# A two-block transformer on one core: inner values of the first mixture turned by VectorE, four lanes in the second mixture, a longer ring of weights

## The chip, the cores and the metric

The kernel runs on one core of one Trainium2 chip. The metric is the device time of an execution in microseconds; before the change the median of three runs is 2532.16 us (2531.34 to 2532.30).

The engines are named as in the profile: PE is TensorE's matmul row and PEld its weight loads, DVE is VectorE, ACT ScalarE, POOL GpSimd, SP SyncE. The queue of SP issues all the loads of weights (SPq).

## What is computed

Two blocks follow each other on 256 tokens of 1024 channels, all in float32: a block of two layers (attention and a dense feed-forward; attention and a mixture of 8 experts with 3584 inner columns, top 2) and a second block (a recurrence and a dilated attention beside each other, then a mixture of 32 experts with 512 inner columns in 4 groups, top 2 within the best group). What the change touches are the two mixtures and what lies just before the second:

```python
def moe_swiglu(h, router_w, w_gate, w_up, w_down):          # first mixture, E = 8, F = 3584
    t = h.reshape(B * S, D)
    logits = (t @ router_w).astype(jnp.float32)
    top_v, top_i = lax.top_k(logits, TOP_K)
    top_w = jax.nn.softmax(top_v, axis=-1)
    gates = jnp.sum(jax.nn.one_hot(top_i, N_EXPERTS) * top_w[..., None], axis=1)
    for e in range(N_EXPERTS):
        y = y + gates[:, e:e + 1] * swiglu(t, w_gate[e], w_up[e], w_down[e])

def swiglu(h, w_gate, w_up, w_down):
    return (jax.nn.silu(h @ w_gate) * (h @ w_up)) @ w_down

def hier_moe(h, ...):                                       # second mixture, E = 32, F = 512
    grp_logits = h @ w_router_group + b_router_group
    grp = jnp.argmax(grp_logits, axis=-1)
    exp_logits = (h @ w_router_expert + b_router_expert).reshape(N, 4, 8)[tok_idx, grp]
    top_v, top_i = lax.top_k(exp_logits, 2)
    gate = softmax(grp_logits)[grp] * jax.nn.softmax(top_v, axis=-1)
    # each token goes through its two experts: (silu(x @ w_gate[e]) * (x @ w_up[e])) @ w_down[e]
```

## The kernel before

Activations are held with channels on the partitions (`x_chan`, `h_chan`: 128 x 8 x 256). Weights come from one stream of slots of 128 x 2048 floats (1.0486 MB) into a ring of 14 slots in SBUF. `Loads.load` (L128) makes SP wait until the slot's last user has counted up `used` and issues one DMA per slot; `Loads.ready` makes the reader wait for the arrival. The order of the loads on SP's queue is the order of the code.

Each stage is a block of five engine programs; a block ends for all engines together. The stages are: setup, mixer 0, dense, mixer 1, route and first mixture (`stage_route` L1097, `stage_blocks` L1490), the hybrid stage (front, attention, recurrence, merge), route and second mixture (`stage_route` again, `stage_lanes` L1806).

**Routing.** `stage_route` scales the activations, multiplies them with the router's weights (L1140), transposes them to tokens on the partitions (L1148, ACT copies them to `h_tok`), finds the first two experts of each token on DVE (L1176 to L1211), and numbers the tokens of each expert (`place`). `fullest` is the number of tokens of the fullest expert. `pick_slots` (L1241) turns places into 0/1 matrices, and a matmul of `h_tok` with them gathers an expert's tokens (L1344, L1704).

**Overflow.** A mixture's main pass gives each expert a fixed width, 96 tokens in the first, 64 in the second. If `fullest` is above it, an `If` in each engine runs all the further rounds of that width up to 256 tokens, each with all the weights again.

**First mixture.** `BlockWork.pe_expert` (L1396) takes one expert at a time. The expert's 96 tokens are three blocks of 32. For each slot of weights TensorE runs 3 x 4 matmuls (L1368), each with 32 tokens as the stationary operand in one quarter of the array's columns, so that partition 32 i + token of a bank holds the inner columns of quarter i. The 3584 inner columns go in two spans, 4 x 512 (slots 0 to 15, gate then up) and 4 x 384 (slots 16 to 31). ACT takes the SiLU, DVE the product (`hidden`, L1479). For the down projection the inner columns must lie on partitions: `pe_flips` (L1373) transposes `hidden` on TensorE in pieces of 128x128, 12 for the wide span and 9 for the narrow one, and DVE copies them from PSUM to `turned` (L1484). The down slots 32 to 45 follow (L1390, 24 matmuls of 256 columns a slot), with the next expert's gather between.

**Second mixture.** `LaneWork.pe_group` (L1719) takes two experts (lanes) at a time, 64 tokens each, in the two halves of the columns: 8 slots of gate and up weights (L1722), a gather for the next group (L1704), 4 transposes of `hidden` (L1733), 4 slots of down weights (L1749), and the spread of the results back to all tokens (L1760), which DVE adds up (L1800). 16 groups use 192 slots; the inner 14 are a loop on each engine. Its ring has 12 of the 14 slots. SP issues the first 12 loads at the start of the second route's block (`loads.head`) and the others in the mixture's block.

**Merge.** `hybrid_merge` (L2527) is the last block ahead of the second route: the two branches are projected (L2559, L2591), gated, and multiplied with `w_out` (L2606, four slots). SP loads the router and the last two `w_out` slots there.

## Time and profile before

| | |
|---|---|
| median of 3 runs | 2532.16 us |
| profiled execution | 2534.23 us |
| its span | 2532.1 us |
| PE busy | 2452.8 us (97%) |
| DVE busy | 768.9 us (30%) |
| ACT busy | 327.4 us (13%) |
| moved from HBM | 716.54 MB |
| mean granted TensorE clock | 0.993 |

The span runs from the first to the last instruction of the profiled execution. A matmul in float32 leaves two records in the trace, a transpose one. PE counts as busy while a matmul is under way, so its share does not say how full the array is; matmuls in different quarters of the columns run beside each other, and their durations add up to more than the busy time. PEclk is the granted clock as a share of 2.4 GHz.

### The profile page before, as it was taken

How to read it: one execution, taken by the hardware profiler on the slowest of the kernel's cores; microseconds unless marked ns; L12 is line 12 of the kernel's file. 1: busy time of each engine (PE TensorE's matmuls, PEld its weight loads, DVE VectorE, ACT ScalarE, POOL GpSimd, SP SyncE). 2: the span in 40 equal slices, each digit the busy share in tenths (PEclk: the TensorE clock that was granted, in tenths of full speed). 3: DMA queues.
4: the chain of work that ended last, by engine and by line, in shares of the span. 5: the costliest groups of instructions: out<-in, count | busy, mean ns of one | idle time of the engine just before them, and what ended most of it. 6: DMA issues, size and time to landing. Idle time of an engine off the chain costs nothing. (4 is left out here: it accounts for less than half of the span.)

```text
span 2532.1 us, 50359 instructions
## 1 busy us (share of the span) xinstructions
PE 2452.8 (97%) x22858; PEld 1545.7 (61%) x22858; DVE 768.9 (30%) x1341; ACT 327.4 (13%) x728; POOL 14.5 (1%) x12
## 2 busy tenths in 40 slices
PE   6999999999999999999999999999999999999999
PEld 5678888867453535353535353688789864444444
DVE  6762222436201010111111111345465342222222
ACT  3430000243100000000000000233232110000000
POOL 1000000100000000000000000000000000000000
PEclk9999999999999999999999999899999999999999
DMA  9566554605699999999999999333300179999998
GB/s 399 212 271 252 216 216 199 251 1 233 244 364 364 369 362 371 361 375 353 378 355 379 357 377 351 136 123 139 130 3 4 37 330 406 422 422 421 422 422 354
DMA packets 105238, 720.68 MB, mean 285 GB/s; under 512 B 11952, under 2 KB 12624, under 8 KB 30416
## 3 DMA queue, kind: packets, MB, share of 16 engines
q1 hardware_dynamic: 105040, 717.67, 71.5%
q8 instruction: 169, 2.77, 0.4%
q14 instruction: 29, 0.24, 0.0%
HBM read 716.54 MB, written 1.05 MB: 283 GB/s over the span
## 5 line engine op out<-in xcount | busy, mean ns | idle before, releaser
L1368 PE MATMUL bank<-ring,moe_xg 128*32 128x512 f32 (+1 forms) x6144 | 582.3, 539 | 6.1 <-DVE moe_acc L1468 5.5
L1368 PEld LDWEIGHTS bank<-ring,moe_xg 128*32 128x32 f32 x6144 | 197.8, 110 | 378.1 <-issue 367.8
L1390 PE MATMUL bank<-ring,moe_turned 128*32 128x256 f32 x5376 | 296.1, 379 | 0.0
L1390 PEld LDWEIGHTS bank<-ring,moe_turned 128*32 128x32 f32 x5376 | 172.3, 110 | 116.1 <-issue 4.4
L1722 PE MATMUL bank<-ring,moe_shared 128*64 128x512 f32 x1024 | 223.5, 594 | 0.8 <-DVE moe_shared L1773 0.8
L1057 PE MATMUL bank<-h_chan,ring 128*128 128x256 f32 x896 | 195.6, 379 | 1.4 <-ACT h_chan L482 1.4
L1057 PEld LDWEIGHTS bank<-h_chan,ring 128*128 128x128 f32 x896 | 170.2, 190 | 24.7 <-issue 1.6
L1722 PEld LDWEIGHTS bank<-ring,moe_shared 128*64 128x64 f32 x1024 | 72.0, 137 | 142.6 <-issue 141.6
L2199 PE MATMUL bank<-h_chan,ring 128*128 128x256 f32 x672 | 149.7, 383 | 1.9 <-DVE h_chan L2304 1.9
L1479 DVE TENSOR_TENSOR moe_hidden<-moe_silu,bank 128x512 f32<-128x512 f32 (+1 forms) x48 | 26.9, 616 | 395.0 <-PE bank L1368 395.0
L2199 PEld LDWEIGHTS bank<-h_chan,ring 128*128 128x128 f32 x672 | 128.2, 192 | 23.6 <-issue 6.3
L1749 PE MATMUL bank<-ring,moe_turned 128*64 128x512 f32 x512 | 113.4, 595 | 0.8 <-DVE moe_turned L1785 0.8
L1041 PE MATMUL bank<-dense_hidden,ring 128*128 128x256 f32 x448 | 98.8, 379 | 0.0
L1041 PEld LDWEIGHTS bank<-dense_hidden,ring 128*128 128x128 f32 x448 | 85.1, 190 | 11.6
L580 PE MATMUL bank<-h_chan,ring 128*128 128x256 f32 x384 | 85.1, 380 | 1.0 <-ACT h_chan L482 1.0
L1454 DVE COPY moe_y<-bank 32x256 f32<-32x256 f32 x48 | 19.9, 415 | 209.5 <-PE bank L1390 209.0
L1437 ACT ACTIVATE moe_silu<-bank 128x512 f32<-128x512 f32 (+1 forms) x48 | 22.6, 544 | 471.0 <-PE bank L1368 471.0
L580 PEld LDWEIGHTS bank<-h_chan,ring 128*128 128x128 f32 x384 | 72.5, 190 | 15.0 <-issue 5.4
L1749 PEld LDWEIGHTS bank<-ring,moe_turned 128*64 128x64 f32 x512 | 35.3, 137 | 66.8 <-issue 64.0
L1447 ACT ACTIVATE moe_y<-bank 32x256 f32<-32x256 f32 x48 | 18.1, 377 | 441.0 <-PE bank L1390 440.5
L1781 DVE TENSOR_TENSOR moe_hidden<-moe_silu,bank 128x512 f32<-128x512 f32 x16 | 11.0, 688 | 201.8 <-PE bank L1722 201.8
L1074 DVE TENSOR_TENSOR dense_hidden<-dense_silu,bank 128x512 f32<-128x512 f32 x14 | 9.6, 687 | 201.3 <-PE bank L1057 201.3
(408 smaller groups left out, 2436.5 us busy)
## 6 DMA issues: line engine op xcount, KB each, us to landing
ring<-stream SPq DMA_DIRECT2D x313, 1024.0 KB, 13.8
ring<-wide SPq DMA_DIRECT2D x240, 1024.0 KB, 7.2
ring<-wide SPq DMA_DIRECT2D x128, 768.0 KB, 6.0
ada_slots<-stream SPq DMA_DIRECT2D x28, 1024.0 KB, 6.9
x_chan<-xT SPq DMA_DIRECT2D x1, 1024.0 KB, 14.9
ring<-lora SPq DMA_DIRECT2D x1, 1024.0 KB, 6.5
out<-x_chan SPq DMA_DIRECT2D x4, 256.0 KB, 2.1
hyb_work<-dilated SPq DMA_DIRECT2D x1, 768.0 KB, 8.9
```

The source lines that it names most:

```text
L580: mm = nc.tensor.matmul(b[:, 0:T], w[:, t, i * P:(i + 1) * P], k.hT[:, t, :], start=(t == 0), stop=(t == DT - 1))
L1041: mm = nc.tensor.matmul(k.bank[t // 2][:, (t % 2) * T:(t % 2) * T + T], w[:, f, t * P:(t + 1) * P], hidden[:, c % 2, f, :], start=(c == 0 ...
L1057: mm = nc.tensor.matmul(b[:, f * T:(f + 1) * T], w[:, t, f * P:(f + 1) * P], k.hT[:, t, :], start=(t == 0), stop=(t == DT - 1))
L1368: mm = self.k.nc.tensor.matmul(banks[r][i * TILE:(i + 1) * TILE, 0:width], self.m.xg[:, t, r * TILE:(r + 1) * TILE], w[:, i, :], start=(t ...
L1390: mm = self.k.nc.tensor.matmul(self.sum_bank[r][q * TILE:(q + 1) * TILE, :], self.m.turned[:, r, 4 * c + f, i * TILE:(i + 1) * TILE], w[:, ...
L1437: k.nc.scalar.activation(m.silu[:, r, 0:self.span[c]], self.gate_bank[r][:, 0:self.span[c]], ACT.Silu)\
L1447: last = self.k.nc.scalar.activation(self.m.y[r * TILE:(r + 1) * TILE, q * T:(q + 1) * T], self.sum_bank[r][q * TILE:(q + 1) * TILE, :], A ...
L1454: last = self.k.nc.vector.tensor_copy(self.m.y[r * TILE:(r + 1) * TILE, q * T:(q + 1) * T], self.sum_bank[r][q * TILE:(q + 1) * TILE, :])
L1479: v.tensor_tensor(m.hidden[:, r, 0:self.span[c]], m.silu[:, r, 0:self.span[c]], self.up_bank[r][:, 0:self.span[c]], ALU.mult).then_inc(*se ...
L1722: mm = k.nc.tensor.matmul((self.gate_bank if j < self.per_proj else self.up_bank)[own, :], m.xg[:, t, own], w[:, i, e, :], start=(t == 0), ...
L1749: mm = k.nc.tensor.matmul(k.bank[half][own, :], m.turned[:, f, own], w[:, i, e, :], start=(f == 0), stop=(f == 3))
L2199: mm = nc.tensor.matmul(b[:, 0:T], lhsT, rhs, start=(t == 0), stop=(t == DT - 1))
```

## The change

- *First mixture.* `pe_flips` is gone. DVE turns `hidden` into `turned` with its own transpose, which turns each block of 32x32 in place of the grid, SBUF to SBUF, one instruction per block of tokens and span. The down weights' rows are put in the order that this gives, on the host. TensorE waits for the products (`hidden_ready`) before the second narrow projection and before down slot 35, and for `turned_ready` where it waited for the copies.
- *Second mixture.* Its width falls from 64 to 32 tokens, so four experts share the array's columns: 8 groups, each with 16 slots of gate and up weights and 8 of down weights, still 192 slots. All groups are written out, with no loop. The overflow rounds are seven instead of three.
- *Ring.* Two more slots (`late`) lie in the memory that the hybrid stage uses as `work`; the second mixture's ring has 16 slots in the order `LAST_ORDER`. SP issues its loads 0 to 14 in the merge's block, between the last loads of the hybrid stage, and load 15 in the route's.
- *Routes.* The logits are computed with the router's weights as the stationary operand (8 matmuls with 256 columns instead of 16), copied by DVE and transposed to tokens in two pieces between the other transposes. `acc` is cleared after the mask, not before the first step. The gate weights move out of the route's block to behind the first gather's copies (`gate_weights`), and the first `pick_slots` moves into it.
- *Merge.* Temporaries lie elsewhere; the arithmetic is the same.

```diff
-RING = 14
+RING, LATE = 14, 2
@@ Loads
-        p = j % self.slots
+        p = self.order[j % self.slots]
@@ stage_route
-                for tok in range(TT):
-                    mm = nc.tensor.matmul(k.bank[1][:, tok * R:(tok + 1) * R], k.hT[:, t, tok * P:(tok + 1) * P],
-                                          router_w[:, t, :], start=(t == 0 and tok == 0), stop=(t == DT - 1),
-                                          skip_group_check=True)
-            mm.then_inc(*pe_step.up())
+                mm = nc.tensor.matmul(k.bank[4][0:R, 0:T], router_w[:, t, :], k.hT[:, t, :], start=(t == 0),
+                                      stop=(t == DT - 1))
+            mm.then_inc(*S("logits_done").up())
...
+                if n == 2:
+                    pe.wait_ge(*S("logits_out").at(1))
+                    for half in range(TT):
+                        mm = nc.tensor.transpose(k.bank[1][:, half * R:(half + 1) * R],
+                                                 logit_rows[:, half * P:(half + 1) * P], k.t("ident")[0:R, 0:R])
+                    mm.then_inc(*pe_step.up())
...
-            link(v.memset(m.acc[:, :, :], 0.0))
+            dve.wait_ge(*S("logits_done").at(1))
+            v.tensor_copy(logit_rows, k.bank[4][0:R, 0:T]).then_inc(*S("logits_out").up())
             dve.wait_ge(*pe_step.at(1))
...
-            dve.wait_ge(*S("exp_done").at(1))
-            link(v.tensor_scalar(col("w1"), col("w"), 1.0, None, ALU.add))
...
-            link(v.tensor_tensor(m.gates[:, :, :], col("hot1", E), col("hot2", E), ALU.add))
+            link(v.memset(m.acc[:, :, :], 0.0))
             dve.wait_ge(*pe_step.at(2))
...
+            pick_slots(k, m, first, link)
@@ BlockWork.pe_expert
-        self.pe_project(pe, g, 16, self.gate_bank, NARROW, range(2))
-        self.pe_flips(pe, g, 0)
-        self.pe_project(pe, g, 16, self.gate_bank, NARROW, range(2, DT))
+        self.pe_project(pe, g, 16, self.gate_bank, NARROW)
+        pe.wait_ge(*self.hidden_ready.at(g * 6 + 3))
         self.pe_project(pe, g, 24, self.up_bank, NARROW)
-        pe.wait_ge(*self.flip_out.at(g * 6 + 3))
+        pe.wait_ge(*self.turned_ready.at(g * 6 + 3))
         for j in range(32, 46):
-            if j == 34:
-                self.pe_flips(pe, g, 1)
+            if j == 35:
+                pe.wait_ge(*self.hidden_ready.at(g * 6 + 6))
...
             if j == 40:
-                pe.wait_ge(*self.flip_out.at(g * 6 + 6))
+                pe.wait_ge(*self.turned_ready.at(g * 6 + 6))
@@ BlockWork.dve_expert
-                dve.wait_ge(*self.flip_done.at(g * 6 + (3 * c + r + 1)))
-                n = self.parts[c]
-                v.tensor_copy(m.turned[:, r, 4 * c:4 * c + n, :], self.flip_bank[3 * c + r][:, 0:n * P].rearrange(
-                    "p (f n) -> p f n", f=n)).then_inc(*self.flip_out.up())
+                dve.wait_ge(*self.hidden_ready.at(g * 6 + (3 * c + r + 1)))
+                f0 = c * WIDE
+                v.transpose(m.turned[:, r, f0:f0 + self.span[c]], m.hidden[:, r, 0:self.span[c]])\
+                    .then_inc(*self.turned_ready.up())
@@ stage_lanes, TensorE
-            main.pe_group(pe, 0, True)
-            main.pe_spread(pe, 0)
-            with pe.Fori(1, G - 1) as g:
-                main.pe_group(pe, g)
-                main.pe_spread(pe, g)
-            main.pe_group(pe, G - 1, False, True)
+            for g in range(G):
+                main.pe_group(pe, g, g == 0, g + 1 == G)
+                if g + 1 < G:
+                    main.pe_spread(pe, g)
@@ hybrid
+LAST_ORDER = [5, 6, 8, 9, 10, 11, 12, 13, RING, RING + 1, 7, 1, 2, 3, 4, 0]
+ISSUED = 15
@@ hybrid_merge, SP
-            for j in range(ATTN_OUT + HYBRID_RING, loads.n):
+            for j in range(4):
+                nxt.load(sp, j)
+            loads.load(sp, ATTN_OUT + HYBRID_RING)
+            for j in range(4, 10):
+                nxt.load(sp, j)
+            sp.wait_ge(*loads.done(ATTN_OUT))
+            nxt.load(sp, 10)
+            for j in range(ATTN_OUT + HYBRID_RING + 1, loads.n):
                 loads.load(sp, j)
+            for j in range(11, ISSUED):
+                nxt.load(sp, j)
@@ program
-                ("hybrid", 31, HYBRID_RING, 1), ("moe2", 12, 12, 16)]
+                ("hybrid", 31, HYBRID_RING, 1), ("moe2", 192, RING + LATE, 1)]
...
-                m = Mixture(k, stage, "moe2", 32, C, "router2", 36, True)
+                m = Mixture(k, stage, "moe2", 32, QUAD_SLOTS, "router2", 36, True,
+                            k.late[:, LATE, :].rearrange("p (t n) -> p t n", t=TT))
@@ host
+def turned_rows(down):
+
+    wide = down[:QUADS * WIDE].reshape(QUADS, WIDE // TILE, TILE, D)
+    narrow = down[QUADS * WIDE:].reshape(QUADS, NARROW // TILE, TILE, D)
+    return np.concatenate([part.transpose(1, 0, 2, 3).reshape(-1, D) for part in (wide, narrow)])
```

TensorE's order in the first mixture, one expert from its wide up projection to its last down slots; before (L1379 are the transposes, L1368 the projections, L1390 the down slots, L1344 the gather):

```order
L1368 MATMUL bank<-ring,moe_xg 32x512 x96
L1368 MATMUL bank<-ring,moe_xg 32x384 x24
L1379 MATMUL bank<-tab_sb,moe_hidden 128x128 x12
L1368 MATMUL bank<-ring,moe_xg 32x384 x168
L1390 MATMUL bank<-ring,moe_turned 32x256 x48
L1379 MATMUL bank<-tab_sb,moe_hidden 128x128 x9
L1390 MATMUL bank<-ring,moe_turned 32x256 x24
L1344 MATMUL bank<-moe_pick,moe_h_tok 128x96 x8
L1390 MATMUL bank<-ring,moe_turned 32x256 x24
```

and now:

```order
L1391 MATMUL bank<-ring,moe_xg 32x512 x96
L1391 MATMUL bank<-ring,moe_xg 32x384 x192
L1402 MATMUL bank<-ring,moe_turned 32x256 x72
L1367 MATMUL bank<-moe_pick,moe_h_tok 128x96 x8
L1402 MATMUL bank<-ring,moe_turned 32x256 x24
```

The two runs of transposes are gone, and the projections and down slots around them close up; nothing else moves.

SyncE's queue from the merge's block to the start of the second mixture's, before (`ring<-stream` is a slot of weights; the first two are `w_out`'s, the twelve belong to the mixture):

```order
L2546 DMA ring<-router 128x288
L2547 DMA ring<-router_b 128x36
L136 DMA ring<-stream 128x2048 x2
L2543 UNCONDITIONAL_BRANCH
L1112 UNCONDITIONAL_BRANCH
L136 DMA ring<-stream 128x2048 x12
L1111 UNCONDITIONAL_BRANCH
```

and now (`late<-stream` are the two new slots; among the seventeen in the merge's block two are `w_out`'s, the fifth and the thirteenth):

```order
L2553 DMA late<-router 128x288
L2554 DMA mod<-router_b 128x36
L138 DMA ring<-stream 128x2048 x9
L138 DMA late<-stream 128x2048 x2
L138 DMA ring<-stream 128x2048 x6
L2550 UNCONDITIONAL_BRANCH
L1123 UNCONDITIONAL_BRANCH
L138 DMA ring<-stream 128x2048
L1122 UNCONDITIONAL_BRANCH
```

Fifteen of the mixture's loads now stand in the merge's block and one in the route's.

TensorE in the second mixture, its first group, before (L1722 gate and up, L1277 gate turns, L1704 gather, L1733 transposes, L1749 down, L1760 spread):

```order
L1722 MATMUL bank<-ring,moe_shared 64x512 x16
L1277 MATMUL bank<-tab_sb,h_chan 128x128 x16
L1722 MATMUL bank<-ring,moe_shared 64x512 x16
L1277 MATMUL bank<-tab_sb,h_chan 128x128 x16
L1704 MATMUL bank<-moe_pick,moe_h_tok 128x128 x8
L1733 MATMUL bank<-tab_sb,moe_hidden 128x128 x4
L1704 MATMUL bank<-moe_pick,moe_h_tok 128x128 x8
L1749 MATMUL bank<-ring,moe_turned 64x512 x16
L1760 MATMUL bank<-moe_gate_t,moe_shared 128x256 x8
```

and now:

```order
L1737 MATMUL bank<-ring,moe_shared 32x512 x32
L1300 MATMUL bank<-tab_sb,h_chan 128x128 x8
L1737 MATMUL bank<-late,moe_shared 32x512 x8
L1737 MATMUL bank<-ring,moe_shared 32x512 x24
L1300 MATMUL bank<-tab_sb,h_chan 128x128 x8
L1719 MATMUL bank<-moe_pick,late 128x128 x8
L1748 MATMUL bank<-tab_sb,moe_hidden 128x128 x4
L1719 MATMUL bank<-moe_pick,late 128x128 x8
L1764 MATMUL bank<-ring,moe_turned 32x512 x32
L1775 MATMUL bank<-moe_gate_t,moe_shared 128x256 x8
```

The gate and up matmuls of a group are 64 of 32 columns where they were 32 of 64, the down matmuls 32 where they were 16; gather, transposes and spread of a group are as many as before, for four experts instead of two.

## Rows read from the trace of the kernel before

**Rows 1.** The page, its head.

```profile
span 2532.1 us, 50359 instructions
```

**Rows 2.** Busy time per engine in stretches (us busy, records; then PEclk, DMA share, GB/s).

```profile
1100.00:1200.00 100.00, 98.78 (x1216) 44.59 (x1219) 10.23 (x18) 5.09 (x12) 0.00 (x0) 1.00 0.94 359
...
2200.00:2300.00 100.00, 100.00 (x511) 47.49 (x511) 25.98 (x39) 1.79 (x3) 0.00 (x0) 1.00 1.01 422
2500.00:2540.00 40.00, 27.21 (x124) 11.35 (x124) 9.89 (x12) 0.60 (x1) 0.00 (x0) 0.97 0.57 232
```

**Rows 3.** SyncE's queue, waits from 700 to 1560 us (total, times, longest).

```profile
SPq L188 <- PE bank L1368: 482.7, 201, 6.6
```

**Rows 4.** TensorE's timeline, first mixture (start, duration, line, operation, count).

```profile
940.22 1.09 PE L1379 MATMUL bank<-tab_sb,moe_hidden 128*128 128x128 f32 x8
...
942.30 27.30 PE L1368 MATMUL bank<-ring,moe_xg 128*32 128x384 f32 x336
...
974.71 1.20 PE L1379 MATMUL bank<-tab_sb,moe_hidden 128*128 128x128 f32 x9
975.84 2.80 PE L1390 MATMUL bank<-ring,moe_turned 128*32 128x256 f32 x48
...
1061.15 1.09 PE L1379 MATMUL bank<-tab_sb,moe_hidden 128*128 128x128 f32 x8
```

**Rows 5.** The chain that ended last, second mixture (start, duration, what).

```profile
2063.83 7.09 PE bank L1722 x32
...
2096.65 13.88 PE bank L1722 x64
...
2125.60 13.88 PE bank L1722 x64
...
2143.68 7.02 PE bank L1749 x32
...
2154.54 13.88 PE bank L1722 x64
```

**Rows 6.** Stretch at the head loads' start.

```profile
2038.00:2040.00 2.00, 1.86 (x16) 1.67 (x15) 1.67 (x1) 0.29 (x1) 0.00 (x0) 1.00 0.38 115
```

**Rows 7.** Groups by line, 1000 to 1100 us (busy us, mean ns of one; idle before).

```profile
L1368 PE MATMUL bank<-ring,moe_xg 128*32 128x512 f32 (+1 forms) x768 | 72.8, 539 | 0.8 <-DVE moe_acc L1468 0.8
...
L1484 DVE COPY moe_turned<-bank 128x512 f32<-128x512 f32 (+1 forms) x6 | 3.5, 619 | 6.9 <-PE bank L1379 6.9
```

**Rows 8.** Timeline of the second route.

```profile
2040.12 3.26 DVE L476 SCALAR_TENSOR_TENSOR h_chan<-x_chan,vec_sb,rstd 128x256 f32<-128x256 f32 x8
...
2043.75 1.76 DVE L1168 MEMSET moe_acc<- 128x2048 f32 x1 [0.38 <-issue]
...
2044.37 3.48 PE L1148 MATMUL bank<-tab_sb,h_chan 128*128 128x128 f32 x16
...
2045.55 0.17 DVE L1191 TENSOR_TENSOR moe_gl<-bank,ring 128x8 f32<-128x8 f32 x1
...
2052.04 0.22 DVE L1211 TENSOR_TENSOR moe_chosen<-moe_hot 128x64 f32<-128x64 f32 x1
...
2057.41 2.93 PE L1704 MATMUL bank<-moe_pick,moe_h_tok 128*128 128x128 f32 x12 [1.03 <-DVE moe_pick L1241]
```

**Rows 9.** Timelines of the merge, SyncE's queue and TensorE.

```profile
1994.45 7.24 SPq L136 DMA_DIRECT2D ring<-stream  x2
...
2008.07 27.79 PE L2606 MATMUL bank<-h_chan,ring 128*128 128x256 f32 x128
```

**Rows 10.** Groups by line, second mixture.

```profile
L1722 PE MATMUL bank<-ring,moe_shared 128*64 128x512 f32 x1024 | 223.5, 594 | 0.8 <-DVE moe_shared L1773 0.8
```

**Rows 11.** Timeline of the kernel's end.

```profile
2525.12 3.72 PE L1889 MATMUL bank<-moe_gate_t,moe_shared 128*128 128x256 f32 x16
```

**Rows 12.** Stretches behind the first mixture.

```profile
1610.00:1615.00 5.00, 2.32 (x37) 1.27 (x26) 2.49 (x6) 2.26 (x6) 0.00 (x0) 0.91 0.02 3
1615.00:1620.00 5.00, 4.63 (x12) 3.49 (x11) 2.08 (x5) 1.81 (x5) 0.00 (x0) 0.50 0.03 7
```

More of the change, by code:

```diff
@@ L115, with __init__ @@
 class Loads:
-    def __init__(self, ring, n, slots=RING, turns=1):
+    def __init__(self, ring, n, slots=RING, turns=1, order=None):
         assert turns == 1 or n % slots == 0
@@ L146, in ready @@
     def ready(self, pe, j, turn=0):
[L148 removed]
+        p = self.order[j % self.slots]
         per = self.n // self.slots if self.turns > 1 else 0
@@ L225, in __init__ @@
         self.ring = sb("ring", [P, RING, SLOT])
-        self.weights = self.new_ring("slot", [self.ring[:, p, :] for p in range(RING)])
+        self.weights = self.new_ring("slot", [self.ring[:, p, :] for p in range(RING)] + [None] * LATE)
         self.used = self.weights.used
@@ L1114, in _ @@
             if loads is not None:
-                loads.head(sp)
+                for j in range(ISSUED, loads.slots):
+                    loads.load(sp, j)
         @block.scalar
@@ L1809, in stage_lanes @@
     W = m.width
-    main = LaneWork(k, m, loads)
+    main = LaneWork(k, m, loads, False)
     G = m.experts // main.lanes
     k.family = family
-    more = [LaneWork(k, m, part) for part in again]
+    more = [LaneWork(k, m, part, True) for part in again]
     first = more[0]
@@ L2524, in hybrid_attention, with hybrid_merge @@
     k.close()
-def hybrid_merge(k, loads, rec, o, fin, gate, acc, nxt_norm):
+def hybrid_merge(k, loads, nxt, rec, o, fin, gate, acc, nxt_norm):
     nc = k.nc
@@ L2991, in program @@
             if RUN is None or name in RUN:
-                loads[name] = Loads(k.weights, n, ring, turns)
+                loads[name] = Loads(k.weights, n, ring, turns, LAST_ORDER if name == "moe2" else None)
                 if name == "ada":
```

150 lines of the change are left out of this document (74 added, 76 removed).

## The prediction

> **What bounds the kernel now.** I read the page first (span, throttle, transfer rate), then the stage table, then TensorE's timeline in the first mixture, the chain of waits in the second, and the joints between. Three stages matter. The profiled execution took 2534.2 us, of which 2532.1 is span [rows 1] and 2.1 lie around it; the median, 2532.2, is 2.1 below it.
>
> The first mixture (646 to 1610 us) is bound by TensorE. Its busy time is 98.8 of 100 us at full clock, beside transfers at 359 GB/s [rows 2], and in 860 us of it SyncE's queue waited 482.7 us for a projection to give a slot back [rows 3]. One expert's first transposes start at 940.22, the next one's at 1061.15: 120.93 us [rows 4], and the same holds for the other inner experts.
>
> The second mixture (2063.8 to 2525) stands close to two limits at once. TensorE's chain has no gap: a group of two experts takes 2154.54 - 2125.60 = 28.94 us [rows 5], and there are 16. The transfers run at 422 GB/s with a DMA share of 1.01 [rows 2], the highest sustained in the trace; a slot of 1.0486 MB is then 2.485 us, and a group's twelve slots 29.8 us. TensorE gets along with less than that only because the twelve slots loaded ahead are slowly used up. The last bytes: 232 GB/s times 40 us is 9.28 MB after 2500 [rows 2], less 1.05 MB of output, so 19.5 us at 422: the last weights land near 2519.5.
>
> Between them the DMA engines are nearly idle, until SyncE's head loads begin to flow about 2039.4 (a DMA share of 0.38 in 2038 to 2040 [rows 6]).
>
> **First mixture.** Removed: 21 TensorE transposes per expert. They cost TensorE 940.22 to 942.30 (12 of them with the wait for the bank between) and 974.71 to 975.84 (9): 2.08 + 1.13 = 3.21 us, times 8 experts = **25.7 us**, all on the path. Also removed are six copies PSUM to SBUF per expert on DVE (619 ns mean [rows 7]).
>
> Added: six DVE transposes of 128x512 or 128x384, SBUF to SBUF. The trace of before has none. From below, the nearest row is that copy, 0.62 us; from above I allow 1.9 us, three times it. The place decides nothing up to far more: the first three have the whole narrow projections, over 30 us, to finish in; the second three start about 2 us after the last projection and must be done by down slot j = 40, eight down slots (2.80 us each [rows 4]) and two gathers after the last projection, some 25 us. Three transposes of up to 7 us each are hidden. I take 0. The two new waits on the products (before the second narrow projection, and at down slot j = 35) come 15 us and 8 us after the matmuls that feed them, while three products, of the copies' size, take some 2 us: 0. Behind DVE's transposes stand only the takes for the next expert, needed 25 us later. The order of the down weights is changed on the host: 0.
>
> With an expert at 117.7 us, the transfers must give 44.04 MB (3 x 1024 x 3584 floats) / 117.7 us = 374 GB/s instead of 364. The projections and down slots already draw faster than that between pauses, and 422 is shown elsewhere [rows 2]; 0.
>
> **Routes.** Logits are now computed turned (8 matmuls of 256 columns for 16 narrow ones), copied and turned back; the gate weights leave the route, the clearing of acc moves behind the mask, the first picks move ahead of the block's end. In the second route DVE's last scaling ended at 2043.38 and its first routing step came at 2045.55, right after the 1.76 us clearing [rows 8]. Now the step follows the last logit matmul (about 2044.2: wait, 0.44 of matmul, landing), half of the sixteen transposes (3.48 / 2 = 1.74 us) and two small ones: about 2046.2, **0.7 us later**. After it, the mask is done 6.7 us later as before (2045.55 to 2052.26), then 1.76 of clearing, 0.9 of places, 0.6 of picks, 1.8 of block change: 11.8 us, against 57.41 - 45.55 = 11.86. So +0.7 us to the first weight matmul, now 2064.5. In the first route the same steps end on TensorE's own queue (turns, ten warming matmuls, mask sums), which do not shrink: 0, bounds -1 and +1.
>
> **Prefetch.** SyncE issues slots 0 to 3 at the merge's start (1982), 4 to 14 between w_out loads, slot 15 in the route: 16 instead of 12, all landed by about 2042. What is passed: the third w_out slot goes out at 1994.45 as before [rows 9], the fourth behind seven mixture slots. Even if all nine land in turn, 1994.5 + 1 + 9 x 2.485 = 2017.9; TensorE reads it after three quarters of 27.79 us, at 2028.9 [rows 9]. 11 us of cover: 0. Without that cover TensorE would wait for it in the merge and everything after would shift.
>
> **Second mixture.** With four lanes of 32 columns, a slot is four matmuls (0.87 us) instead of 1.74, if four narrow matmuls overlap as two wide ones did. The first mixture's do: a record of 448 columns in the mean costs it 72.8 / 768 = 0.095 us [rows 7], or 0.108 at 512, half of the second's 223.5 / 1024 = 0.218 with two lanes [rows 10]; a matmul leaves two records, so a slot is 8 x 0.108. A group now covers four experts and 24 slots, and TensorE needs for it again 28.94 us (13.88 up, 7.02 down, the rest gathers, turns, spread [rows 5]) while its transfers take 24 x 2.485 = 59.6. So the **transfers alone** set the end. Gather, spread and DVE halve behind them: 0. The refill begins when the first slot is free, 2064.5 + 0.87 = 2065.4, flows 1.5 us later (as the head did: route block 2037.9, flow 2039.4), and has 192 - 16 = 176 slots: 437.4 us, last landing 2504.3. Before, it was 2519.5. The last slot then costs 0.87 us and the tail 6.98 (2525.12 to 2532.1 [rows 11]) at full clock.
>
> The clock: after a stretch with TensorE busy 2.32 of 5 us the granted clock was 0.91, then 0.50 in the next 5 [rows 12]; 0.50 is 1.2 GHz. In the new stage TensorE has 0.87 us of work in each 2.485, so I expect 1.2 GHz near the end: the last slot 1.74 instead of 0.87, and two tail steps 0.9 more together. End 2504.3 + 0.1 + 1.7 + 7.9 = 2514.0, a gain of **18.1 us** in this stage with the route's 0.7 in it.
>
> [...]
>
> **Sum.** 2532.1 - 25.7 - 18.1 = 2488.3 span, 2490.4 for the profiled execution; for the median the two offsets of 2.1 cancel: **2488.3 us**.
>
> **Rivals.**
> 1. *The first mixture turns transfer-bound.* For it: share 0.94 at 359 GB/s [rows 2], as if little were left. Against: SyncE waits on TensorE, not the reverse [rows 3]. If so, the 25.7 us stay: 2514.
> 2. *TensorE at 1.2 GHz through the whole second mixture.* A group then takes 57.9 us, just under 59.6, so it never works off the lead: first group (2063.83 to 2096.65 before, 32.8 us, with the gate turns [rows 5]) 65.5, six groups 347.4, the last 44: 2064.5 + 457 = 2521.4, plus 7.9, less 25.7: about 2504. For it [rows 12]; against, full clock should return when work is dense.
> 3. *The other side: an expert with more than 32 tokens.* The width of the second mixture's main pass falls from 64 to 32; if any expert draws 33 or more, all seven overflow rounds run, each at least 192 slots of 2.485 us: 7 x 477 = 3340 us more, 5830 in all. The trace cannot show the fullest expert, only that it is at most 64. Working out the reference's routing for its own inputs gives 26 for the fullest of 32 (mean 16), which speaks strongly against it.
>
> **Chances.** Forecast 0.78, rival 1 0.06, rival 2 0.12, rival 3 0.04. A measurement of this kernel tells about 0.2% (5 us) from no change; none of the first three comes within that. Range: full clock at the end (-1.8), 425 instead of 422 GB/s (-3), routes (-1) and rounding give 2481; rival 2 gives 2504. Rivals 1 and 3 stay outside. Faster 0.94, within 0.2% 0.02, slower 0.04.
>
> **What would show it.** First mixture: expert to expert 117.7 us; DVE transposes well under 7 us with TensorE waiting for none. Merge: DMA share high from 1982, w_out matmuls still 27.8 us. Second mixture: 422 GB/s up to the last landing, groups 59.6 us apart, TensorE waiting on ring slots, the clock at 0.5 in parts. Wrong if the expert period stays near 120.9, if the transfers fall below 415 GB/s (each 1% is 4.4 us), or if overflow rounds appear.

## The result, and the profile after

The changed kernel takes **2486.4 us** (median of 4 runs, 2483.5 to 2489.9), the kernel before 2531.8 beside it (4 runs, 2530.9 to 2532.3): a ratio of 0.9822, with a 95% interval of 0.9805 to 0.9839. The forecast was 2488.3 in a range of 2481 to 2504. The profiled execution is the slowest of the four, 2489.9 us with a span of 2487.8; against the span of [rows 1] that is 44.3 us less, where the forecast had 43.8. The two numbers agree better than their parts do, so the parts come first.

The page of the changed kernel: its span, and in 40 slices TensorE's busy tenths, its granted clock, and the transfer rate.

```profile
span 2487.8 us, 47996 instructions
...
PE   6999999999999999999999999999999987776776
...
PEclk9999999999999999999999999999999998777777
...
GB/s 398 224 253 279 220 220 203 256 1 188 241 381 367 387 372 387 364 387 371 386 367 388 370 385 364 141 125 135 124 3 4 255 184 420 421 421 421 422 421 332
```

The first mixture (slices 12 to 25) still shows a full TensorE, now at 364 to 388 GB/s. In the last seven slices, the second mixture, TensorE is idle for a fifth to two fifths of the time, its clock is at seven or eight tenths, and the transfers stand at 421 until the last slice: what bounds the stage has changed hands.

The same in stretches, to be laid beside [rows 2] (us busy and records of TensorE, its weight loads, VectorE, ScalarE, GpSimd; granted clock, DMA share, GB/s):

```profile
1100.00:1200.00 100.00, 99.22 (x1216) 41.30 (x1204) 11.85 (x22) 5.09 (x12) 0.00 (x0) 1.00 0.97 379
2200.00:2300.00 100.00, 71.56 (x408) 22.18 (x400) 11.40 (x17) 0.60 (x1) 0.00 (x0) 0.76 1.01 421
```

TensorE's timeline over one inner expert of the first mixture, which answers to [rows 4] (start, duration, line, operation, count):

```profile
880.32 20.78 PE L1391 MATMUL bank<-ring,moe_xg 128*32 128x512 f32 x192
901.03 3.91 PE L1380 MATMUL bank<-moe_gate_t,moe_y 96*128 96x256 f32 x16
905.73 51.77 PE L1391 MATMUL bank<-ring,moe_xg 128*32 128x512 f32 x576 [0.79 <-DVE moe_acc L1479]
957.31 7.95 PE L1402 MATMUL bank<-ring,moe_turned 128*32 128x256 f32 x144
...
971.83 26.11 PE L1402 MATMUL bank<-ring,moe_turned 128*32 128x256 f32 x480
997.75 2.76 PE L1391 MATMUL bank<-ring,moe_xg 128*32 128x512 f32 x24
```

From 905.73 to 957.31 the projections run in one piece; before, 12 transposes with a wait stood in them, and 9 more in the down slots. An expert now takes 997.75 - 880.32 = 117.43 us, against 120.93: 3.50 us less. From the first gather to the closing products the eight experts took 968.1 us before and 940.1 now, 28.0 less. SyncE's queue still waits for TensorE and not the other way round; its waits from 700 to 1530 us (total, times, longest) answer to [rows 3]:

```profile
SPq L190 <- PE bank L1391: 464.5, 199, 6.6
```

What VectorE does in TensorE's place, grouped by line and shape from 700 to 1500 us (busy us, mean ns of one; idle before):

```profile
L1495 DVE STREAM_TRANSPOSE moe_turned<-moe_hidden 128x512 f32<-128x512 f32 x18 | 11.3, 682 | 0.0
L1490 DVE TENSOR_TENSOR moe_hidden<-moe_silu,bank 128x512 f32<-128x512 f32 x18 | 11.3, 683 | 125.6 <-PE bank L1391 125.6
```

A turn of 128x512 in 32x32 blocks takes 682 ns, as long as the product before it (128x384: 547 ns), and waits for nothing. The forecast's bounds for it were 0.62 and 1.9 us.

The end of the kernel, which answers to [rows 11] (start, duration, engine and operation, idle before and what ended it):

```profile
2471.91 1.77 PE L1764 MATMUL bank<-ring,moe_turned 128*32 128x512 f32 x8 [0.53 <-DMA ring<-stream]
...
2474.34 1.06 PE L1764 MATMUL bank<-ring,moe_turned 128*32 128x512 f32 x8 [0.66 <-DMA ring<-stream]
2475.47 0.69 DVE L1808 COPY moe_shared<-bank 128x512 f32<-128x512 f32 x1 [9.16 <-PE bank L1764]
...
2478.18 6.39 PE L1898 MATMUL bank<-moe_gate_t,moe_shared 128*128 128x256 f32 x16 [2.78 <-issue]
```

Two things are new here. Between the last slot and the closing products (line 1898) TensorE stands for 2.78 us and waits for nothing that the profile shows. And these products take 6.39 us instead of the 3.72 of [rows 11], the same 16 records.

**Where the 44.3 us lie**, by the starts of the same steps in the two traces:

| stretch | forecast | measured |
|---|---|---|
| start to the first gather of the first mixture (646.39, now 643.53) | 0 | -2.9 |
| eight experts of the first mixture | -25.7 | -28.0 |
| its closing products and the norm behind | 0 | -4.4 |
| hybrid stage up to the merge (mostly the recurrence) | 0 | +2.4 |
| merge and second route up to the first weight product | +0.7 | -0.4 |
| second mixture and tail | -18.8 | -11.0 |

The -4.4 are a clock: the eight closing products (16 records) take 3.72 us now, and 2.93 and 4.42 us in two pieces before, when the granted clock fell to 0.50 [rows 12]. They are not shown to belong to the change: in kernels with the change's code at this place the same products took 3.7, 5.4, 6.9 or 7.1 us. The +2.4 and the shortfall in the last row needed experiments.

### The profile page after: what moved, and what is told of

It reads as the page before. It is cut to its first block and busy times, and to the rows that moved or that the text cites. A ratio compares the mean times of both kernels' runs of the same rounds, so it can differ in the third digit from the quotient of the medians.

```text
span 2487.8 us, 47996 instructions
## 1 busy us (share of the span) xinstructions
PE 2289.4 (92%) x22230; PEld 1400.9 (56%) x22230; DVE 708.9 (28%) x1263; ACT 320.1 (13%) x716; POOL 14.5 (1%) x12
## 3 DMA queue, kind: packets, MB, share of 16 engines
q8 instruction: 178, 2.92, 0.5%
## 5 line engine op out<-in xcount | busy, mean ns | idle before, releaser
L1737 PE MATMUL bank<-ring,moe_shared 128*32 128x512 f32 x896 | 161.7, 818 | 79.6 <-DMA ring<-stream 78.8
L1737 PEld LDWEIGHTS bank<-ring,moe_shared 128*32 128x32 f32 x896 | 22.1, 123 | 210.2 <-DMA ring<-stream 196.0
L1764 PE MATMUL bank<-ring,moe_turned 128*32 128x512 f32 x448 | 71.1, 736 | 36.8 <-DMA ring<-stream 36.8
L1796 DVE TENSOR_TENSOR moe_hidden<-moe_silu,bank 128x512 f32<-128x512 f32 x8 | 5.5, 688 | 250.4 <-PE bank L1737 250.4
L312 DVE CUSTOM_DVE_ANT_0 ada_product<-ada_slots,ada_c 128x1024 f32<-128x1024 f32 x56 | 68.5, 1223 | 1.5
```

What stands on the lines that cost most here:

```text
L312: mul = k.nc.vector.tensor_tensor_reduce(product, w[:, i * D:(i + 1) * D], c_row, 1.0, 0.0, ALU.mult, ALU.add, accum_out=k.mod[:, l, at:at ...
L1737: mm = k.nc.tensor.matmul((self.gate_bank if j < self.per_proj else self.up_bank)[own, :], m.xg[:, t, own], w[:, i, e, :], start=(t == 0), ...
L1764: mm = k.nc.tensor.matmul(k.bank[half][own, :], m.turned[:, f, own], w[:, i, e, :], start=(f == 0), stop=(f == 3))
```

## Experiments

All have before measured beside them; "the change" is the changed kernel.

**1. The first mixture alone.** The kernel before with the new first mixture and its down weights; all else as it was.

```
+ v.transpose(m.turned[:, r, f0:f0 + span], m.hidden[:, r, 0:span])
- self.pe_flips(pe, g, 0)   (and the copies out of the flip banks)
+ turned_rows(down[e])      (the host's order of the down weights)
```

> The kernel before, with the new first mixture alone: inner values turned by the vector engine in 32x32 blocks, down weights in that order, no TensorE transposes; routes, merge and second mixture as before. If the gain of the first mixture is TensorE's own (the transposes it no longer issues, 28.0 us less in the trace of the change), it comes out here alone: 2503 to 2507 us, a ratio of 0.989 to 0.990. If the first mixture were bound by its transfers, or if its gain hung on the new route, this would stay at 2530 or above 2510. The 2.4 us that the change lost in the recurrence should be absent if they come from the changed buffers of the hybrid stage, and present if they come from where instructions lie in memory.

Measured: 2501.6 us (2500.5 to 2503.4), ratio 0.9884 (0.9868 to 0.9901), 29.9 us less, 1.4 us better than the range expected. The projections are in one piece again, and the eight experts take 940.1 us, as in the change. It is the larger part of the change and stands by itself. The recurrence took 352.0 us here, with the old buffers, so the changed buffers are not what makes it long.

```profile
907.08 51.77 PE L1368 MATMUL bank<-ring,moe_xg 128*32 128x512 f32 x576 [0.78 <-DVE moe_acc L1456]
```

**2 to 4. The loads ahead and the lanes, apart.** First, all sixteen first slots asked for in the route:

```
-ISSUED = 15
+ISSUED = 0        (and no nxt.load in hybrid_merge)
```

> The change without its loads ahead: none of the sixteen first slots of the second mixture is asked for in the merge, all sixteen at the start of the second route. If the second mixture is set by its transfers, all 192 slots then follow that point: 192 x 2.49 us from about 2009 us gives a last landing near 2487 instead of 2474 us, and a time of 2497 to 2500 us. If the merge's own wait gets shorter without those loads in its way, up to 4 us of it come back. If TensorE were the bound of the second mixture, nothing but the first slot's landing would count, and the time would stay within 2 us of the change, 2486.

Then eight of them in the merge:

```
-ISSUED = 15
+ISSUED = 8
```

> The change with only eight of the slots of the second mixture asked for in the merge and eight at the start of the second route. The route's 23 us hold the transfer of eight slots (8 x 2.49 = 19.9 us and a landing of about 2 us), so all sixteen are in when the first slot comes free: no change, 2484 to 2489 us. If instead every slot asked for in the merge counts, half of the loss of the kernel without loads ahead appears, about 6 us: 2492.

Then two lanes with the loads ahead:

```
-QUAD_SLOTS = 32
+QUAD_SLOTS = 64   (two late slots given up for tables)
```

> The change with two lanes of 64 tokens in place of four lanes of 32 in the second mixture, with the loads ahead kept (thirteen of fourteen slots, since the wider tables take the room of the two late slots). If TensorE's 28.94 us a group of twelve slots sets the pace again, sixteen groups take 463.0 us, and with the new start at 2030.6 and a tail of 6 to 10 us the time is 2499 to 2504 us. If the loads ahead alone made the gain and lanes did nothing, 2486 to 2489.

Measured: without loads ahead 2496.9 (ratio 0.9870, 0.9854 to 0.9887); eight ahead 2486.2 (0.9825, 0.9808 to 0.9841), the change's time; two lanes 2501.1 (0.9882, 0.9865 to 0.9898). The four kernels that have the new first mixture, side by side, medians in us (all but the first have the new routes too):

| | two lanes | four lanes |
|---|---|---|
| no loads ahead | 2501.6 | 2496.9 |
| loads ahead | 2501.1 | 2486.4 |

The first kernel has the old routes, and these alone cost it 3.0 us ahead of the first gather (see the routes below). So the 0.5 and 4.7 us that separate it from the next two are not the worth of loads or lanes. The traces tell them apart, by the time from the second mixture's first weight product to the end, in us:

| | two lanes | four lanes |
|---|---|---|
| no loads ahead | 468.3 | 468.8 |
| loads ahead | 470.6 | 457.2 |

The kernel before takes 468.3 there. Neither part gains anything alone; together they gain 11. The chain that ended last says why. In the two-lane kernel, from 2150 to 2200 us (start, duration, what), it is TensorE without a gap, a group every 29.00 us, so an earlier transfer has nothing to bring:

```profile
2149.99 13.88 PE bank L1737 x64
2163.87 1.98 PE bank L1719 x16
2168.08 7.02 PE bank L1764 x32
2177.03 1.97 PE bank L1775 x8
2178.99 13.88 PE bank L1737 x64
```

In the kernel without loads ahead it is the transfers. They run at 1.02 from before TensorE's first slot on, and all 192 slots lie behind the route's start; from the second gather to the last slot it takes 461.6 us, against 448.6 in the change. What the four lanes free before the last landing is lost again behind it: from the last slot's start to the end this kernel takes 12.1 us, where the kernel before takes some 8.7 (an estimate, with the start put at the last quarter of its 7.09 us of down products). Its stretches:

```profile
2020.00:2040.00 20.00, 18.35 (x156) 8.49 (x154) 7.54 (x17) 2.93 (x4) 0.00 (x0) 0.96 1.02 422
2040.00:2460.00 420.00, 301.63 (x1716) 89.27 (x1716) 50.04 (x71) 5.26 (x9) 0.00 (x0) 0.77 1.01 421
```

And eight slots ahead are as good as fifteen, because the route's 23 us move the other eight before TensorE gives the first one back. What counts is that sixteen have landed by then, not when they were asked for.

**5. The change again**, beside the next three on one chip.

> The changed kernel as it is, again, beside the next three on the same chip. 2483 to 2490 us. If the 2.4 us that its recurrence took longer (352.5 us from the first input product of the hybrid stage to the first product of the merge, against 350.1 before) belong to the change, it is 352 to 353 again; if it is a spread of the executions, anything from 348 to 353. The gap between the last slot and the closing products is again 1.7 to 2.8 us.

Measured: 2484.7 us (2483.8 to 2485.2), ratio 0.9814. The recurrence took 350.4 us, so the same kernel has it at 352.5 and at 350.4. Over all kernels with this very code it took 348.2 to 352.5 us. The +2.4 of the table are such a spread, not the change. Three TensorE gaps of 0.22 to 0.36 us put down to "issue", which this trace lacks, make 0.9 of the 2.0 us between the two; what makes them and the rest is open. The gap ahead of the closing products is there again, 2.92 us, just above the range expected.

**6 to 8. Who makes the gap?** Three edits on TensorE's queue. Twelve identity products ahead of the branch on the fullest expert:

```
+ keep_warm(k, k.bank[5], 12)
  with pe.If(fullest > W):
```

> The change with twelve identity products (128x128, 0.24 us each at the full clock) on TensorE between the last slot's products and the branch on the fullest expert. If the 2.8 us gap there is TensorE's sequencer at the branch while its array has nothing to do, and the 6.40 us of the closing products are the clock that fell in that gap, the filler runs inside the gap and the closing products take 3.7 us: about 2.7 us less than the change, 2483 to 2484. If the branch is decided only after the array has finished what is ahead of it, the filler adds its 2.9 us and the gap stays: 2487 to 2490.

TensorE's branch left out:

```
- with pe.If(fullest > W):
-     ...
```

> The change with TensorE's branch after the last group left out, and with it TensorE's part of the rounds for experts with more than 32 tokens, which these inputs do not need (the fullest has 26). If the gap before the closing products is the branch, reached only when the last slot has landed, it goes: the first closing products start within 0.1 us of the last slot's end, and the time from there to the end falls from 12.4 us to about 7 at the full clock or 9.6 at the half: 2.8 to 5.4 us less than the change, 2481 to 2484. If the gap is the vector engine's copy of the last sums, only the order inside the 12.4 us changes: 0 to 1 us less.

The branch ahead of the last group's down slots:

```
+ with pe.If(fullest > W):  down slots; extra rounds; closing products
+ with pe.Else():           down slots; closing products
```

> The change with TensorE's branch moved ahead of the last group's eight down slots: both sides of the branch hold those slots and the closing products, and the one for full experts also the extra rounds, so nothing is left out. The branch then costs its 2 to 3 us where TensorE idles 0.5 to 1.4 us a slot for transfers anyway and catches up within a few slots. Same as with the branch left out: 2.8 to 5.4 us less than the change, 2481 to 2484. If an Else costs a jump before the closing products too, or code has to be fetched there, the gap stays and it is no faster than the change.

Measured: filler 2488.0 us (2484.0 to 2489.6), no branch **2479.1** (2477.8 to 2483.9; 5.6 less than experiment 5, a little more than expected), early branch 2485.3 (2481.9 to 2486.2). TensorE's timelines, of the kernel with the filler, without the branch, and with the early branch:

```profile
2468.93 1.93 PE L1764 MATMUL bank<-ring,moe_turned 128*32 128x512 f32 x8 [1.38 <-DMA ring<-stream]
2470.80 5.03 PE L302 MATMUL bank<-tab_sb 128*128 128x128 f32 x24
2476.22 3.72 PE L1899 MATMUL bank<-moe_gate_t,moe_shared 128*128 128x256 f32 x16 [0.39 <-issue]
```

```profile
2469.95 1.72 PE L1764 MATMUL bank<-ring,moe_turned 128*32 128x512 f32 x8 [0.51 <-DMA ring<-stream]
2471.60 3.72 PE L1877 MATMUL bank<-moe_gate_t,moe_shared 128*128 128x256 f32 x16
```

```profile
2463.83 3.57 PE L1769 MATMUL bank<-late,moe_turned 128*32 128x512 f32 x16 [7.07 <-issue]
...
2473.80 1.76 PE L1769 MATMUL bank<-ring,moe_turned 128*32 128x512 f32 x8 [1.40 <-DMA ring<-stream]
2475.49 4.67 PE L1912 MATMUL bank<-moe_gate_t,moe_shared 128*128 128x256 f32 x16
```

The gap is the branch with the code that it passes over: without them the closing products follow the last slot at once and take 3.72 us. VectorE's copy of the last sums, the other reading, is still there and delays nothing. The filler did run inside the gap (0.39 us of it are left) and restored the clock, but itself took 5.03 us at the lower level. So that expectation was half right: the reading of the gap holds, the price of the filler did not, and the median of 2488.0 us lies where the expectation had put the opposite reading. The trace decides, not the median. Moved forward, the branch costs more, 7.07 us, and most of it is caught up; from the second gather to the end it is 459.3 us against 461.9 in experiment 5 and 457.0 without the branch. Those 2.6 us are not shown to be the edit's: in experiment 12, whose second mixture is the change's own code, the same stretch took 458.8 us. The 457.0 without the branch do lie below all traces of that code (458.8 to 462.1). The median doesn't show a gain either: in this kernel's profile the products that close the first mixture took 7.1 us instead of 3.7.

**9 to 10. Where the branch can hide.** First the sides changed, so that the side taken lies right behind it:

```
- with pe.If(fullest > W):        extra rounds' side
- with pe.Else():                 the side taken
+ with pe.If(fullest < W + 1):    the side taken
+ with pe.Else():                 extra rounds' side
```

> As the kernel with the early branch, but with the sides changed: the side that these inputs take lies right behind the branch, and the extra rounds lie behind it as the other side, so no jump over them stands ahead of the closing products. If the 2.9 us (behind the last slot) and 7.1 us (ahead of the down slots) at the branch were the jump over the extra rounds' code, the gap ahead of the down slots falls under 1 us and the stretch from the second gather to the end falls from 461.9 to about 457 us as with the branch left out: 2479 to 2482 us in all. If it is the branch itself, whichever way it goes, the gap ahead of the down slots stays at several us and the stretch at 459: 2482 to 2486.

Then the sides as in the early branch, but the whole last group in both:

> As the kernel with the early branch, but with TensorE's branch ahead of the last group's sixteen projection slots, so that both sides hold the whole group and 24 slots lie behind the branch. Its 7 us then come out of the 0.5 to 1.4 us that TensorE idles in each slot, and no jump stands at the end of the side that is taken, which in the kernel with the sides changed ended 2.8 us after the last bytes of the result. From the second gather to the end 457 to 458 us, as with the branch left out, and with it a median of 2479 to 2482 us. If 16 slots of the ring are too little to bridge 7 us (transfers stop while TensorE stands), the last landing comes up to 5 us later, and it is no faster than the change, 2484 to 2487.

Measured: 2484.5 (2481.1 to 2484.9) and 2482.9 us (2481.6 to 2483.8), both above the 2479 to 2482 that were expected of a mere jump and of a hidden branch. With the sides changed, the branch itself costs nothing to see (the group's first down slot waits 0.90 us for VectorE, against 0.78 without a branch there), and the closing products follow the last slot as without the branch; but the kernel ends 4.8 us after VectorE's last sum, at 2477.86, where it was 2.5 us without the branch; its last bytes left near 2479.8, 2.9 us before the end. What is left to do there is TensorE's jump over the extra rounds. The profile names the output's transfer for that wait, so that it is the jump is my reading, not shown. From the second gather to the end it is 459.4 us, as with the early branch, not the 457 expected of a jump alone. Ahead of the last group the branch costs 5.19 us, and 24 slots absorb it; the transfers went on at 410 GB/s while TensorE stood, from 2417.5 to 2422.7:

```profile
2413.05 4.50 PE L1780 MATMUL bank<-moe_gate_t,moe_shared 128*128 128x256 f32 x16
2422.75 3.64 PE L1737 MATMUL bank<-late,moe_shared 128*32 128x512 f32 x16 [5.19 <-issue]
...
2470.72 1.77 PE L1769 MATMUL bank<-ring,moe_turned 128*32 128x512 f32 x8 [0.49 <-DMA ring<-stream]
2472.42 3.72 PE L1915 MATMUL bank<-moe_gate_t,moe_shared 128*128 128x256 f32 x16
```

From the second gather to the end this is 457.1 us, the same as without the branch, with all of the change's work kept, and 1.7 to 5.0 us less than in the kernels with the change's own code. The medians don't prove it: 2482.9 against 2484.7, on another chip whose runs of before were 2529.8 instead of 2532.7, so both ratios are 0.9814. By one trace each I take it as the better form of the change; that it is faster is not shown by the medians.

**11. Filler in every slot.**

```
  mm.then_inc(loads.ring.used, 1)
+ keep_warm(k, k.bank[6], 2)     (bank 5 in the down slots)
```

> The change with two identity products (128x128, 0.24 us each at the full clock) behind every slot's products in the second mixture. If TensorE's clock there falls because the engine idles 1.43 us of every 2.49, the filler keeps it at the full level: granted clock near 1.00 in the second mixture, slots of 1.06 + 0.48 us, and since the transfers set the pace no change but in the closing products: 2482 to 2485 us. If the clock alternates as before, a slot at the half level takes 1.94 + 0.86 = 2.80 us, more than the 2.49 of its transfer, and the time rises by up to 0.3 us for each such slot: 2490 to 2520.

Measured: 2484.9 us (2484.2 to 2486.1). TensorE over three slots in it, and its clock in the middle of the stage:

```profile
2204.10 1.06 PE L1738 MATMUL bank<-ring,moe_shared 128*32 128x512 f32 x8 [0.79 <-DMA ring<-stream]
2205.10 0.71 PE L302 MATMUL bank<-tab_sb 128*128 128x128 f32 x4
2206.58 1.07 PE L1738 MATMUL bank<-ring,moe_shared 128*32 128x512 f32 x8 [0.77 <-DMA ring<-stream]
...
2200.00:2300.00 100.00, 82.09 (x584) 40.72 (x584) 13.63 (x20) 0.60 (x1) 0.00 (x0) 1.00 1.01 421
```

Against the change at the same rate of transfer:

```profile
2127.42 1.06 PE L1737 MATMUL bank<-ring,moe_shared 128*32 128x512 f32 x8 [1.42 <-DMA ring<-stream]
2129.91 1.06 PE L1737 MATMUL bank<-ring,moe_shared 128*32 128x512 f32 x8 [1.43 <-DMA ring<-stream]
2132.40 1.94 PE L1737 MATMUL bank<-ring,moe_shared 128*32 128x512 f32 x8 [1.42 <-DMA ring<-stream]
2134.88 1.93 PE L1737 MATMUL bank<-ring,moe_shared 128*32 128x512 f32 x8 [0.55 <-DMA ring<-stream]
```

In the change the slots come in spells, some at 2.4 GHz (1.06 us) and some at 1.2 (1.94); with the filler all are at 2.4, and the time is the same. The gap at the branch is there with the filler too, 1.96 us. The clock of this stage is a symptom: slots start 2.48 us apart either way, because the transfers do.

**12. The turns, three times over.**

```
+ for _ in range(2):
+     link(v.transpose(m.turned[...], m.hidden[...]))
  v.transpose(m.turned[...], m.hidden[...])
```

> The change with each 32x32-block turn of the vector engine in the first mixture done three times (96 more turns, 48 of 0.68 and 48 of 0.55 us, 59 us of work in all, and each with its own semaphore round). If the turns lie hidden beside TensorE's products of the narrow columns, as the prediction has it, the time stays: 2483 to 2488 us. If they are on the way to the down products, each expert gets 7.4 us longer, some 59 us in all: 2540.

Measured: 2483.0 us (2480.6 to 2486.2). The eight experts take 940.1 us again. VectorE is busy 19.6 instead of 11.9 us in the same stretch of the first mixture, TensorE the same 99.22:

```profile
1100.00:1200.00 100.00, 99.22 (x1198) 41.92 (x1191) 19.58 (x34) 5.10 (x12) 0.00 (x0) 1.00 0.97 379
```

## Why the prediction was right, point by point

**First mixture, -25.7.** Right in mechanism and place: the transposes were TensorE's own time (experiment 1), VectorE's turns are hidden (experiment 12), and it did not become transfer-bound, at 0.97 and 379 GB/s. The term is 2.3 us too small. It counted the transposes' own rows, 3.21 us; the expert got 3.50 shorter. The other 0.29 us were not in the sum; that they are what each cut into the projections costs beside its rows is argued, not shown.

**Routes, 0 and +0.7.** The first was argued to be unchanged, within 1 us, because turns, warming products and mask sums "do not shrink". This step is wrong: from the first router product to the first gather the old route takes 14.95 us, in the kernel before and in experiment 1, and the new one 11.9 us in all twelve kernels that have it. Of these 3.0 us, 2.2 are the clock during the turns and warming products. TensorE before and now, with stretches that show the granted clock (the third number from the end):

```profile
635.60 3.65 PE L1148 MATMUL bank<-tab_sb,h_chan 128*128 128x128 f32 x16
639.04 3.46 PE L293 MATMUL bank<-tab_sb 128*128 128x128 f32 x20
...
634.00:638.00 4.00, 4.00 (x23) 4.00 (x23) 3.56 (x12) 1.21 (x3) 0.00 (x0) 0.55 0.00 0
```

```profile
635.17 1.09 PE L1164 MATMUL bank<-tab_sb,h_chan 128*128 128x128 f32 x8
...
637.34 2.40 PE L302 MATMUL bank<-tab_sb 128*128 128x128 f32 x20
...
632.00:636.00 4.00, 4.00 (x23) 2.00 (x22) 2.21 (x6) 2.50 (x7) 0.00 (x0) 1.00 0.01 4
636.00:640.00 4.00, 4.00 (x36) 3.63 (x34) 2.68 (x16) 3.52 (x6) 0.00 (x0) 1.00 0.00 0
```

Before, the clock fell behind router products of 8 columns; now these have 256, and it stays at 1.00. The rest is the router products themselves (4.2 us before, 3.6 now) and the way from the mask sums to the gather. The -2.9 of the table is this, with 0.2 us of spread ahead of it.

In the second route the gather came 1.2 us later, which looks like the +0.7, but the step that the forecast priced did not come later: from the merge's first product to the mask sums it took 70.5 us before and 70.6 now. The delay lies behind the mask, where the forecast had no change: TensorE's own sums and warming products ran at a clock of 0.50 from 2020 to 2025 us, and the gather waited for them, not for VectorE's picks. This stretch took from 4.8 to 6.2 us in kernels with the same code. The gather after it ran at the full clock, 4.05 us instead of 5.63, -1.6 from there to the first weight product; experiment 1, with the old code, had that too. So the -0.4 of the table is a sum of clock spells, not of edits.

**Loads ahead.** Right: w_out is not delayed (the merge's 64 products, 128 records, take 27.79 us again, with and without the loads ahead), and sixteen slots are in before the first is free. Experiment 3 adds that the merge need carry only half of them.

**Second mixture, transfers alone set the end.** Right, and the largest claim in doubt before: neighbouring groups lie 2216.78 - 2157.12 = 59.7 us apart on the chain, forecast 59.6, at 421 GB/s, and lanes and loads ahead only work together (experiments 2 to 4). The step mis-sized is the end of it, by 7.7 us. From the first slot freed to the last slot's product it took 442.7 us, forecast 438.9. The flow began 1.7 us after (forecast 1.5), 176 slots at 421 instead of 422 GB/s are 438.4, and then the last megabyte tapered off, which the forecast let run at the full rate: 0.94 MB in 3.9 us is 1.7 us more than at 421, and 0.9 us passed from there to the product. The changed kernel's transfers at the end:

```profile
2470.00:2471.00 1.00, 1.00 (x8) 0.00 (x0) 0.00 (x0) 0.00 (x0) 0.00 (x0) 0.50 0.79 328
2471.00:2472.00 1.00, 0.47 (x8) 0.09 (x8) 0.00 (x0) 0.00 (x0) 0.00 (x0) 0.50 0.68 287
2472.00:2473.00 1.00, 1.00 (x8) 0.11 (x8) 0.00 (x0) 0.00 (x0) 0.00 (x0) 0.50 0.55 229
2473.00:2474.00 1.00, 0.68 (x4) 0.00 (x0) 0.00 (x0) 0.00 (x0) 0.00 (x0) 0.81 0.24 98
```

The other 3.8 us are the tail: 13.5 us from the last slot's start, forecast 9.7 (1.74 and 7.9, with 0.1). The last slot ran at the full clock, 1.06 us, 0.7 less than forecast. The gap at the branch, 2.8 us, was not in the sum. From the closing products' start to the end it took 9.6 us, where the forecast had the 6.98 of before and 0.9 for the clock: 1.7 too little. Without the branch (experiment 7) all of this is 8.7 us, so branch and clock together are what the forecast had wrong at the end.

The forecast took it that the branch stays free. Before, the closing products followed the last slot without a gap [rows 11], though the branch stood there too, and so they did in the two-lane kernel (experiment 4): in both TensorE was the bound. My reading is that TensorE's sequencer ran ahead of its array there and decided the branch while products still ran, and that now it stands at each slot's landing and reaches the branch after the last one. The filler supports that: with products between the last slot and the branch, 0.39 us of the gap were left. What no run separates is the length of the code: the kernels without a gap (before, and experiments 1 and 4) have three overflow rounds behind the branch, all those with one have seven.

**The rivals.** A first mixture bound by transfers: excluded. TensorE at 1.2 GHz throughout: the mean clock from 2040 to 2460 us was 0.78, and experiment 11 shows that even removing the low spells changes nothing. The Trainium skill (TensorE: Matmul & The Clock Gate, HAM oscillation) tells of a kernel whose clock is throttled again at every DMA wait. The waits that it gives there are 3 to 5 us, behind bursts of about 2 us. Those here are 0.5 to 1.4 us, and the clock fell in spells of several slots, not at each wait; no run here has the page's case. In this stage the low clock cost time only at the end, in 6.39 us of closing products. An expert over 32 tokens: the time shows that none is.

The total came out 0.5 us from the forecast's difference by luck: 10.7 us of gains that it had not named (2.9, 2.3, 4.4 and 1.1) met 10.1 us of losses (2.4 and 7.7). Of the gains only the first two are shown to be the change's; the stretches of the 4.4, of the 1.1 and of the loss of 2.4 differ by 3.2, 1.6 and 4.3 us between kernels with the same code. By the medians the gain is 45.4 us against 43.9 forecast.

## What to carry to other kernels

When two limits of a stage lie close together, price both edits together: lifting one alone gives at most the distance to the other. Here the last stage took 468.8 and 470.6 us with one of them and 457.2 with both, from 468.3. When variants differ in more than one edit, compare the stretch that the edit touches before the medians: here a route that was worth 3.0 us hid in the medians. When a stage changes from engine-bound to transfer-bound, look again at everything that was free because the engine's queue was full: branches and small waits behind the last landing can come onto the path. Put a branch where the engine has slack behind it, and check both its ends: with the sides changed the wait at the branch went, and 2.9 us came up behind the last bytes.

## What the runs showed of the hardware

- A branch on TensorE over a long body, right behind the last slot: from that slot's start to the closing products 3.4 to 4.0 us passed in six traces (experiments 2, 3, 5, 11 and 12 and the first profile of the change), against 1.65 to 1.7 without a branch there (7 to 10). TensorE stood for 1.6 to 2.9 us of it, least where the slot's own products ran at the half clock. As a jump to an Else elsewhere it stood for 7.07 and 5.19 us, and for 0.1 us where the engine falls through the branch.
- VectorE's 32x32-block turn of f32 from SBUF to SBUF costs what a product of that shape does: 682 ns for 128x512, 547 for 128x384.
- Two identity products in each 2.48 us slot hold TensorE's granted clock at 1.00 where it is 0.78 in the mean without them; the transfers ran at 421 GB/s and the time was the same either way.
- Products behind a pause of 2.7 us, the eight that close the first mixture, took 3.7, 5.4, 6.9 or 7.1 us in kernels with the same code there. That, the recurrence's 348 to 352 us and the 458.8 to 462.1 us from the second gather to the end are differences that kernels with the same code show. They are of the size of the 6.4 us over which the changed kernel's own runs spread; that they make it is not shown, since only the profiled executions have a trace. A difference under 3 us between variants can rest on neither a median nor a single stretch here.
- The rate of the transfers held at 421 GB/s almost to the end: over the last four microseconds of the stream their share fell from 1.01 to 0.79, 0.68, 0.55 and 0.24.
